# Sums of squares for eight unit norms: one plain f32 product, or two rounded passes

## The chip, the cores and the metric

The kernel runs on one core of one Trainium2 chip. The metric is the device time of one execution in microseconds, the median of several runs; lower is better. TensorE (PE) multiplies, VectorE (DVE), ScalarE (ACT) and GpSimd (POOL) do element work, SyncE (SP) issues most of the loads. Each engine takes its instructions strictly in the order in which the program lists them, and engines wait for each other by semaphores.

## The reference, cut to what matters

The model is a trunk of two layers over 512 tokens of width 1024. In each layer a combined projection feeds three token mixers, among them a gated delta rule (branch B) with four heads of 128. Its queries and keys go through a short convolution and SiLU, and then each head's vector of each token is scaled to unit length:

```
def l2_norm(x):
    return x * rsqrt(sum(x * x, axis=-1) + EPS)
...
qkv = causal_conv_silu(concatenate([b_q, b_k, b_v]), gdn_conv)
qb = l2_norm(qb.reshape(bsz, seq, B_HEADS, B_HEAD_DIM))
kb = l2_norm(kb.reshape(bsz, seq, B_HEADS, B_HEAD_DIM))
```

Four heads of keys and four of queries make eight unit norms per layer, 16 in all. After them come the delta rule, the other mixers' work, the merge and a squared-ReLU MLP.

## The kernel before, in words

Activations lie transposed: channels on the 128 partitions, the 512 tokens along the free dimension. A head of keys or queries is thus one 128x512 tile, `qkv[:, j, :]`, with j from 0 to 7, and the sum over its 128 channels is a sum over partitions. TensorE does it: a 128x128 matrix of ones times the 128x512 tile of squares gives the sum in every partition at once.

The large products are split in three rounded passes. A weight slab (128x1024) is loaded by SP into `raw`, rounded to `w_hi` (type fp32r) by POOL (lines 1182 and 1183), and VectorE takes the rest `w_lo = raw - w_hi` (line 1081, the step named `lo`); activations have `a_hi` and `a_lo` alike. A product is then hi\*hi + hi\*lo + lo\*hi in fp32r (lines 1216 to 1218), 24 matmuls a slab. The unit norms were not split in this way: line 1357 multiplies plain f32 operands.

The order of all instructions is written out by `schedule()`. The part around the change is its `prefix`, listed by hand. After the convolutions it runs, on each engine in this order (a step does nothing on an engine that has no part in it):

- `unit_sq 0`, `unit_sq 1`, `decays` (a table load on ScalarE, then four small activations and five small VectorE operations), `lo 15`, `rot 0`, `lo 16`, `va_turn`, `gcum`;
- four rounds. Round 0 is `rot 1`, `lo 17`, `unit 0`, `unit_sq 2`, `unit 1`, `unit_sq 3`, `turn 0`, `rows`; rounds 1 and 2 are the same with `rot 2` and `rot 3`, `lo 18` and `lo 19`, units 2, 3 and 4, 5, squares 4, 5 and 6, 7, `turn 1` and `turn 2`; round 3 has the slab `cv 0`, `lo 20`, units 6 and 7, `rot 4`, `turn 3`, and then the slab `cv 1` follows.

What the steps do. `rot r`: TensorE multiplies a slab into a PSUM bank, VectorE multiplies it by a cosine table (line 2159), and ScalarE copies it with its halves exchanged, in four pieces (line 1734), after VectorE's cosine of the same slab. `unit_sq j`: ScalarE squares tile j into `sqs[:, j % 2, :]` (line 1741). `unit j`: TensorE's product (line 1357, waits for the square), ScalarE's Ln and Exp (lines 1749 and 1751), VectorE's multiplication of the tile by the result (line 2174). `turn r`: VectorE multiplies the exchanged copy by a sine table and adds (lines 2168 and 2170). `lo n` makes the `w_lo` of slab n, two slabs ahead; TensorE waits for it before slab n. Slab 15 is that of `rot 1`, 16 that of `rot 2`, 17 that of `rot 3`, 18 and 19 those of `cv 0` and `cv 1`.

`sig(ins, name)` lets an instruction count up a semaphore, and `own(name)` makes an engine wait until its own last instruction of that name has finished.

Of the kernel before, what the change touches and what calls it, by code (L numbers as in the profile page):

```python
# [22 lines left out]
F32R = mybir.dt.float32r  # L23
ALU = mybir.AluOpType
ACT = mybir.ActivationFunctionType
AX = mybir.AxisListType

P = 128
D = 1024
S = 512  # L30
# [8 lines left out]
EPS = 1e-6  # L39
# [645 lines left out]
def build(nc, ws, wo, wd, par, post, tab, x_in, out, rows_d, mt_d, x_d, xt_d):  # L685
    with ExitStack() as ctx:
        def sb(name, shape, dt=F32, where=ctx):
            return where.enter_context(nc.sbuf_tensor(name, shape, dt))
# [9 lines left out]
        def sem(name):  # L698
            if name not in sems:
                sems[name] = ctx.enter_context(nc.semaphore(name))  # L700
            return sems[name]

        def inc(name, n=1, times=1):
            counted[name] += n * times
            return sem(name), n

        def on(name, v, of=None):


            return sem(name), v + (per_layer[name] * (layer if of is None else of) if name in per_layer else before[name])  # L710
# [16 lines left out]
        sqs = sb("sqs", [P, 2, S])  # L727
# [4 lines left out]
        with ExitStack() as mix:  # L732
            qkv = sb("qkv", [P, CONVS, S], where=mix)
            qa = sb("qa", [P, H, S], where=mix)
            ka = sb("ka", [P, S], where=mix)
            va = sb("va", [P, ST, P], where=mix)
            iq = sb("iq", [P, H, S], where=mix)
            ik = sb("ik", [P, S], where=mix)
            oc = sb("oc", [P, H, S], where=mix)
            bw = sb("bw", [P, 10, S], where=mix)  # L740
            tabs2 = sb("tabs2", [P, NTAB - basics], where=mix)
            with ExitStack() as u:
                cqk = sb("cqk", [P, 4, S], where=u)
                cv = sb("cv", [P, ST, S], where=u)
                rp = sb("rp", [P, 2, S], where=u)
            with ExitStack() as u:
                sc = sb("sc", [P, S], where=u)
                work = sb("work", [P, S], where=u)
                rl = sb("rl", [P, 2, S], where=u)
                negb = sb("negb", [P, S], where=u)  # L750
                pr = sb("pr", [P, H, S], where=u)
                pt = sb("pt", [P, 2, S], where=u)
            with ExitStack() as u:
                y_hi = sb("y_hi", [P, H, S], F32R, where=u)
                y_lo = sb("y_lo", [P, H, S], F32R, where=u)
                mt = sb("mt", [P, 3, S], where=u)
# [16 lines left out]
        def T(name, i=0, w=None):  # L773
            a, n = TAB[name]
            w = w or n
            if a < basics:
                return tabs[:, a + i * w:a + (i + 1) * w]
            return tabs2[:, a - basics + i * w:a - basics + (i + 1) * w]
# [82 lines left out]
        def signals(eng, who):  # L861
            seen = seen_by[who]

            def sig(ins, name):
                seen[name] = seen.get(name, 0) + 1
                ins.then_inc(*inc(name))

            def own(name):

                eng.wait_ge(sem(name), seen[name])  # L870

            sig.seen = seen
            return seen, sig, own


        MT, AT = [bw[:, n, :] for n in range(ST)], [bw[:, ST + n, :] for n in range(ST)]
# [113 lines left out]
        def level_count(n, l):  # L990

            return (LEVELS - FIRST) * (n // 2) + l - FIRST + 1

        def drained(name):

            k, a = name[0], name[1:]
            if k == "gcum":
                return [("gc", 1)]
            if k == "unit":
                return [("unit_ln", a[0] + 1)]  # L1000
            if k == "misc_turn":
                return [("misc_in", 3)]
            if k == "va_turn":
                return [("va_in", 1)]
            if k == "rs":
                return [("ret_p", RET[a] + 1)]
            if k == "ro":
                return [("oc", a[0] + 1)]
            if k == "rows":
                return [("rows_T", 1)]  # L1010
            if k == "kk":
                return [("MT", a[0] + 1)]
            if k == "kq":
                return [("AT", a[0] + 1)]
            if k == "kn":
                return [("K", a[0] + 1)]
            if k == "vn":
                return [("vb", a[0] + 1)]
            if k == "p1":
                return [(f"P1{a[0] % 2}", level_count(*a))]  # L1020
            if k == "xx":
                return [(f"X{a[0] % 2}", (LEVELS - 1 - FIRST) * (a[0] // 2) + a[1] - FIRST + 1)]
            if k == "xt":
                return [(f"XT{a[0] % 2}", level_count(*a))]
            if k == "wT":
                return [("wTn", a[0])]
            if k == "v2":
                return [("vnew", a[0] + 1)]
            if k == "oT":
                return [("ob", a[0] + 1)]  # L1030
            if k == "st":
                return [("St", a[0] + 1)]
            if k == "il":
                return [("relu", LOGITS[a[0]] + a[1] + 1)]
            if k == "as":
                return [("smax", H * TURN[a[0]] + a[1] + 1)]
            if k == "pt":
                return [("pt", SPREAD[a[0]] + a[1] + 1)]
            if k == "ao":
                return [("oa", TURN[a[0]] + 1)]  # L1040
            if k == "fin":
                return [("fin_ln", FIN[a])]
            raise ValueError(name)
# [52 lines left out]
        with nc.Block() as block:  # L1096
# [53 lines left out]
            for layer in range(DEPTH):  # L1150
# [63 lines left out]
                def _(pe):  # L1214
# [46 lines left out]
                    def small_bank(name):  # L1261
                        b, _, before = MID[name]
                        if before is not None:

                            for s, v in drained(before):
                                pe.wait_ge(*on(s, v))
                        return psM[b]

                    def small_done(ins):
                        ins.then_inc(*inc("small_done", 1))  # L1270
# [81 lines left out]
                    def unit(j):  # L1352
                        if j == 0:
                            pe.wait_ge(kept["tables_in"], 16 * (layer + 1))
                        pe.wait_ge(*on("unit_sq", j + 1))
                        ps = small_bank(("unit", j))
                        small_done(pe.matmul(ps[:, :], T("ones"), sqs[:, j % 2, :], start=True, stop=True))

                    def cv_tiles(i, ts):
                        u = DENSE["cv", 0]  # L1360
# [310 lines left out]
                def _(act):  # L1671
                    seen, sig, own = signals(act, "act")
# [64 lines left out]
                    def unit_sq(j):  # L1737
                        if j >= 2:
                            mid(act, ("unit", j - 2))
                        act.wait_ge(*on("silu", j + 1))  # L1740
                        sig(act.activation(sqs[:, j % 2, :], qkv[:, j, :], ACT.Square), "unit_sq")

                    def unit(j):
                        ps = mid(act, ("unit", j))
                        if j >= 2:
                            act.wait_ge(*on("unit_done", j - 1))
                        rt = gt[:, 2 + j % 2, :]

                        sig(act.activation(rt, ps[:, :], ACT.Ln, bias=4 * EPS), "unit_ln")
                        own("unit_ln")  # L1750
                        sig(act.activation(rt, rt, ACT.Exp, scale=-0.5,
                                           bias=0.0 if j < H else float(-0.5 * np.log(P))), "unit_r")

# [325 lines left out]
                def _(dve):  # L2079
                    seen, sig, own = signals(dve, "dve")  # L2080
                    total, rstd, diagonal, scaled = dve_norm(dve, sig, own)

                    def f32(ap):
                        return ap.bitcast(F32)
# [76 lines left out]
                    def turn(r):  # L2161
# [7 lines left out]
                        own("rot_sin")  # L2169
                        sig(dve.tensor_tensor(dst, dst, other, ALU.add), "rot_done")  # L2170

                    def unit(j):
                        dve.wait_ge(*on("unit_r", j + 1))
                        sig(dve.tensor_tensor(qkv[:, j, :], qkv[:, j, :], gt[:, 2 + j % 2, :], ALU.mult), "unit_done")

                    def rp_(h, m):
# [224 lines left out]
                    def merge(br, j):  # L2401
# [11 lines left out]
                        for i in range(2):  # L2413
# [2 lines left out]

                    steps = {"norm": norm, "conv": conv, "silu": silu, "misc_turn": misc_turn, "decays": decays, "gcum": gcum,
                             "rot": rot, "turn": turn,
                             "unit": unit, "rp": rp_, "lasts": lasts, "decay": decay, "vb": vb_, "MT": mt_, "AT": at_, "solve": solve,
                             "lev": lev, "Kp": kp_, "Kpp": kpp, "lvl": lvl, "X": x_, "XT": xt_, "Sd": sd, "St": st_,  # L2420
                             "lo": lambda n: lo_slab(dve, n), "index": index, "top": top, "smax": smax, "rinv": recip, "fin": fin,
                             "split": split_y,
# [266 lines left out]
```

## Time and profile before

| | |
|---|---|
| median of 3 runs | 1866.88 us (1866.54 to 1868.51) |
| the profiled execution's own time | 1864.98 us |
| its span, first to last instruction | 1862.8 us |
| busy: PE, DVE, ACT, POOL | 1836.6, 1249.1, 755.3, 265.4 us |
| granted TensorE clock, mean | 0.999 of full |

The profile comes from one execution. Times in it are microseconds from the first instruction. A row of a timeline gives the start, the length, the engine, line and operation, what it writes and reads, and how many instructions are merged in the row; brackets give the idle time of the engine ahead of it and what ended that. A matmul's length reaches into the next matmul, so the pace of matmuls is read from start to start. The same holds for short runs of ACT and DVE instructions that don't depend on each other.

### The profile page before, as it was taken

How to read it: one execution, taken by the hardware profiler on the slowest of the kernel's cores; microseconds unless marked ns; L12 is line 12 of the kernel's file. 1: busy time of each engine (PE TensorE's matmuls, PEld its weight loads, DVE VectorE, ACT ScalarE, POOL GpSimd, SP SyncE). 2: the span in 40 equal slices, each digit the busy share in tenths (PEclk: the TensorE clock that was granted, in tenths of full speed). 3: DMA queues.
4: the chain of work that ended last, by engine and by line, in shares of the span. 5: the costliest groups of instructions: out<-in, count | busy, mean ns of one | idle time of the engine just before them, and what ended most of it. 6: DMA issues, size and time to landing. Idle time of an engine off the chain costs nothing.

```text
span 1862.8 us, 23401 instructions
## 1 busy us (share of the span) xinstructions
PE 1836.6 (99%) x8622; PEld 1484.5 (80%) x8622; DVE 1249.1 (67%) x2064; ACT 755.3 (41%) x1261; POOL 265.4 (14%) x385
## 2 busy tenths in 40 slices
PE   8999999999999999999999999999999999999998
PEld 6877767888888888888778777678887888888886
DVE  6856789854475667575878658897534756575758
ACT  3163343421334636354531533524213346354454
POOL 2221111111120010000012211111112200100000
PEclk9999999999999999999999999999999999999999
DMA  6432213322341794766532322133224308857654
GB/s 247 139 125 85 69 57 99 82 84 68 132 162 46 208 256 133 206 177 174 161 108 91 128 70 79 58 99 86 68 80 176 140 24 239 235 141 198 186 142 102
DMA packets 87039, 240.32 MB, mean 129 GB/s; under 512 B 19920, under 2 KB 32400, under 8 KB 85904
## 3 DMA queue, kind: packets, MB, share of 16 engines
q1 hardware_dynamic: 46656, 171.89, 27.0%
q0 software_dynamic: 10368, 37.75, 10.9%
q10 hardware_dynamic: 29904, 29.19, 4.7%
q8 instruction: 70, 1.15, 0.2%
q14 instruction: 41, 0.34, 0.1%
HBM read 227.75 MB, written 11.06 MB: 128 GB/s over the span
## 4 chain that ended last, share of the span: by engine, by line
PE 90%; DVE 3%; ACT 3%; issue 1%; DMA 1%; ACTq 0%; POOL 0%; DVEq 0%; SPq 0%
PE psD L1216 23%; PE psD L1218 23%; PE psD L1217 23%; PE psM L1216 3%; PE psM L1217 3%; PE psM L1218 3%; PE psM L1275 2%; DMA d_raw<-in_wd 1%; PE psM L1289 1%; PE psM L1484 1%; PE psM L1282 1%; PE psM L1502 1%; PE psM L1381 1%; PE psM L1490 1%; PE psM L1373 1%
## 5 line engine op out<-in xcount | busy, mean ns | idle before, releaser
L1216 PE MATMUL psD<-a_hi,w_hi 128*128 128x512 f32 (+2 forms) x1488 | 594.0, 399 | 0.9 <-DVE w_lo L1081 0.6
L1218 PE MATMUL psD<-a_hi,w_lo 128*128 128x512 f32 (+2 forms) x1488 | 575.2, 387 | 0.0
L1217 PE MATMUL psD<-a_lo,w_hi 128*128 128x512 f32 (+2 forms) x1488 | 574.1, 386 | 0.0
L1081 DVE TENSOR_TENSOR w_lo<-raw,w_hi 128x1024 fp32r<-128x1024 f32 x216 | 264.4, 1225 | 141.3 <-POOL w_hi L1183 96.6
L1216 PEld LDWEIGHTS psD<-a_hi,w_hi 128*128 128x128 f32 (+1 forms) x1488 | 279.0, 188 | 77.8 <-issue 21.1
L1218 PEld LDWEIGHTS psD<-a_hi,w_lo 128*128 128x128 f32 (+1 forms) x1488 | 278.8, 187 | 58.0
L1217 PEld LDWEIGHTS psD<-a_lo,w_hi 128*128 128x128 f32 (+1 forms) x1488 | 279.3, 188 | 56.4 <-issue 4.3
L2496 DVE TENSOR_TENSOR d_lo<-d_raw,d_hi 128x1024 fp32r<-128x1024 f32 x102 | 124.1, 1222 | 69.6 <-ACT d_hi L2029 68.3
L1183 POOL TENSOR_SCALAR w_hi<-raw 128x1023 fp32r<-128x1023 f32 x150 | 166.4, 1109 | 0.0
L1182 POOL TENSOR_TENSOR w_hi<-raw,tabs 128x1 fp32r<-128x1 f32 x150 | 34.7, 231 | 902.6 <-PE psD L1218 871.6
L1190 POOL DMA_DIRECT2D d_raw<-in_wd x72 | 63.4, 956 | 642.7 <-DMA d_raw<-in_wd 435.8
L2029 ACT CAST d_hi<-d_raw 128x1024 fp32r<-128x1024 f32 x102 | 106.0, 1047 | 104.7 <-PE psM L1218 42.7
L2015 ACT CAST w_hi<-raw 128x1024 fp32r<-128x1024 f32 x62 | 65.1, 1050 | 84.1 <-PE psD L1218 83.5
L1216 PE MATMUL psM<-d_hi,f_hi 128*128 128x512 f32 x240 | 94.3, 393 | 0.1
L1218 PE MATMUL psM<-d_hi,f_lo 128*128 128x512 f32 x240 | 93.4, 389 | 0.0
L1217 PE MATMUL psM<-d_lo,f_hi 128*128 128x512 f32 x240 | 93.4, 389 | 0.0
L1931 ACT ACTIVATE gt<-psD 128x512 f32<-128x512 f32 x32 | 19.1, 597 | 159.6 <-PE psD L1218 147.8
L1734 ACT COPY wide<-psD 32x512 f32<-32x512 f32 (+1 forms) x84 | 48.6, 579 | 78.9 <-DVE iq L2159 34.5
L1216 PE MATMUL psD<-y_hi,w_hi 128*128 128x512 f32 x192 | 76.5, 399 | 0.0
L1218 PE MATMUL psD<-y_hi,w_lo 128*128 128x512 f32 x192 | 74.8, 389 | 0.0
L1217 PE MATMUL psD<-y_lo,w_hi 128*128 128x512 f32 x192 | 74.7, 389 | 0.0
L2023 ACT CAST f_hi<-gt 128x768 fp32r<-128x768 f32 x64 | 60.6, 947 | 29.1 <-DVE gt L2484 27.9
(297 smaller groups left out, 2875.7 us busy)
## 6 DMA issues: line engine op xcount, KB each, us to landing
raw<-in_ws SPq DMA_DIRECT2D x216, 512.0 KB, 3.4
d_raw<-in_wd SPq DMA_DIRECT2D x88, 512.0 KB, 5.7
d_raw<-in_wd POOLq DMA_DIRECT2D x72, 512.0 KB, 8.8
s_raw<-in_wo ACTq DMA_DIRECT2D x14, 512.0 KB, 11.5
tabs<-in_tab SPq DMA_DIRECT2D x2, 2944.0 KB, 12.1
x<-rows_d ACTq DMA_DIRECT2D x4, 1024.0 KB, 5.8
x<-out ACTq DMA_DIRECT2D x2, 2048.0 KB, 8.1
x<-in_x SPq DMA_DIRECT2D x4, 512.0 KB, 5.1
```

What stands on the lines that cost most here:

```text
L1081: dve.tensor_tensor(w_lo[:, s, :], raw[:, s, :], w_hi[:, s, :].bitcast(F32), ALU.subtract) \
L1183: pool.tensor_scalar(w_hi[:, s, 1:], raw[:, s, 1:], 1.0, 1.0, ALU.mult, ALU.mult) \
L1190: pool.dma_start(home(name), down_slab(c, b, j), accum_op=ALU.add).then_inc(*inc("sum_" + name[:None if name[0] == "C" else 1], 16))
L1216: pe.matmul(out, lhi, rhi, start=start, stop=False, skip_group_check=more)
L1217: pe.matmul(out, lhi, rlo, start=False, stop=False, skip_group_check=more)
L1218: return pe.matmul(out, llo, rhi, start=False, stop=stop, skip_group_check=more)
L1275: ins = pe.matmul(ps[:, cut(h)], lhs(h), rhs(h), start=True, stop=True)
L1734: sig(act.copy(wt[to:to + n, 6 + r % 2, :], src[at:at + n, :]), "rot_copy" if to + n == P else "rot_part")
L2015: act.copy(w_hi[:, s, :], raw[:, s, :]).then_inc(sem("w_hi"), 1)
L2023: sig(act.copy(f_hi[:, p, w, :], fr[:, w, :]), "f_hi" + part)
L2029: sig(act.copy(operand(c, st)[0], source(st)), "d_hi")
L2496: sig(dve.tensor_tensor(lo, source(st), f32(hi), ALU.subtract), "d_lo")
```

## The change

The squares are split like the other operands, and the sum is made in two passes with a rounded matrix of ones.

- ScalarE: behind each square, after waiting for it, a cast of the squares to `sq_hi` (fp32r). Both count on `unit_sq`.
- VectorE: a new step `unit_sq` in the place that the order already had for it: it waits for the cast and subtracts, `sq_lo = sqs - sq_hi`. Once per layer it also copies the ones to `ones_r`.
- TensorE: `unit j` waits for `sq_lo` of j, and then multiplies `ones_r` by `sq_hi` and by `sq_lo` into the same bank.
- The new tiles lie where `cv` and `rp` lie later. The Ln now counts on the same semaphore as the Exp (`unit_r`), and the waits' numbers follow.

```
+                sq_hi = sb("sq_hi", [P, 2, S], F32R, where=u)
+                sq_lo = sb("sq_lo", [P, 2, S], F32R, where=u)
+                ones_r = sb("ones_r", [P, P], F32R, where=u)
...
             if k == "unit":
-                return [("unit_ln", a[0] + 1)]
+                return [("unit_r", 2 * a[0] + 1)]
...
                     def unit(j):
-                        pe.wait_ge(*on("unit_sq", j + 1))
+                        pe.wait_ge(*on("unit_lo", j + 2))
                         ps = small_bank(("unit", j))
-                        small_done(pe.matmul(ps[:, :], T("ones"), sqs[:, j % 2, :], start=True, stop=True))
+                        pe.matmul(ps[:, :], ones_r[:], sq_hi[:, j % 2, :], start=True, stop=False)
+                        small_done(pe.matmul(ps[:, :], ones_r[:], sq_lo[:, j % 2, :], start=False, stop=True))
...
                         sig(act.activation(sqs[:, j % 2, :], qkv[:, j, :], ACT.Square), "unit_sq")
+                        own("unit_sq")
+                        sig(act.copy(sq_hi[:, j % 2, :], sqs[:, j % 2, :]), "unit_sq")
...
+                    def unit_sq(j):
+                        dve.wait_ge(*on("unit_sq", 2 * j + 2))
+                        if j == 0:
+                            sig(dve.tensor_copy(ones_r[:], T("ones")), "unit_lo")
+                        sig(dve.tensor_tensor(sq_lo[:, j % 2, :], sqs[:, j % 2, :], f32(sq_hi[:, j % 2, :]), ALU.subtract),
+                            "unit_lo")
+
                     def unit(j):
-                        dve.wait_ge(*on("unit_r", j + 1))
+                        dve.wait_ge(*on("unit_r", 2 * j + 2))
```

## Rows read from the trace of the kernel before

**Rows 1.** The page: busy time of each engine; engines on the last chain.
```profile
PE 1836.6 (99%) x8622; PEld 1484.5 (80%) x8622; DVE 1249.1 (67%) x2064; ACT 755.3 (41%) x1261; POOL 265.4 (14%) x385
...
PE 90%; DVE 3%; ACT 3%; issue 1%; DMA 1%; ACTq 0%; POOL 0%; DVEq 0%; SPq 0%
```

**Rows 2.** PE's waits, whole span: total us, times, longest us.
```profile
PE psM L1357 <- ACT sqs L1741: 1.1, 2, 0.5
...
PE psD L1216 <- DVE w_lo L1081: 0.6, 2, 0.3
```

**Rows 3.** Timeline of PE, layer 0, from rot 1 to units 6 and 7.
```profile
100.58 0.47 PE L1216 MATMUL psD<-a_hi,w_hi 128*128 128x512 f32 x1 [0.31 <-DVE w_lo L1081]
...
113.23 0.39 PE L1218 MATMUL psD<-a_hi,w_lo 128*128 128x512 f32 x1
113.46 1.88 PE L1357 MATMUL psM<-sqs,tabs 128*128 128x512 f32 x4
...
115.40 0.39 PE L1217 MATMUL psD<-a_lo,w_hi 128*128 128x512 f32 x1
...
129.76 1.13 PE L1357 MATMUL psM<-sqs,tabs 128*128 128x512 f32 x2 [0.54 <-ACT sqs L1741]
```

**Rows 4.** Timeline of ACT, layer 0: the first squares, then one round.
```profile
95.31 1.14 ACT L1741 ACTIVATE sqs<-qkv 128x512 f32<-128x512 f32 x2
96.47 1.28 ACT L1700 ACT_TABLE_LOAD   x1
...
107.06 2.39 ACT L1734 COPY wide<-psD 32x512 f32<-32x512 f32 x4 [2.99 <-DVE cqk L2159]
109.47 0.60 ACT L1749 ACTIVATE gt<-psM 128x512 f32<-128x512 f32 x1
110.10 0.63 ACT L1751 ACTIVATE gt<-gt 128x512 f32<-128x512 f32 x1
110.64 0.61 ACT L1741 ACTIVATE sqs<-qkv 128x512 f32<-128x512 f32 x1
111.16 0.58 ACT L1749 ACTIVATE gt<-psM 128x512 f32<-128x512 f32 x1
...
112.31 0.62 ACT L1741 ACTIVATE sqs<-qkv 128x512 f32<-128x512 f32 x1
...
115.09 2.38 ACT L1734 COPY wide<-psD 32x512 f32<-32x512 f32 x4 [2.03 <-DVE cqk L2159]
```

**Rows 5.** Timeline of DVE, layer 0: decays, lo 15, end of round 0, turn 1.
```profile
98.46 0.17 DVE L2136 SCALAR_TENSOR_TENSOR small<-small 128x16 f32<-128x16 f32 x1 [2.33 <-ACT small L1706]
...
99.21 1.22 DVE L1081 TENSOR_TENSOR w_lo<-raw,w_hi 128x1024 fp32r<-128x1024 f32 x1
...
112.43 0.69 DVE L2174 TENSOR_TENSOR qkv<-qkv,gt 128x512 f32<-128x512 f32 x1 [0.97 <-ACT gt L1751]
113.04 0.69 DVE L2168 TENSOR_TENSOR wide<-wide,tabs 128x512 f32<-128x512 f32 x1
...
114.37 0.68 DVE L2159 TENSOR_TENSOR cqk<-psD,tabs 128x512 f32<-128x512 f32 x1
...
121.80 1.42 DVE L2170 TENSOR_TENSOR cqk<-cqk,wide 128x512 f32<-128x512 f32 x1
```

**Rows 6.** Tile y_hi: a cast and a subtraction; ns min/median/max, first and last start.
```profile
L1897 ACT CAST y_hi<-oc x8: 613/616/619, 378.3 to 1304.9; 128x512 fp32r<-128x512 f32 x8
...
L2373 DVE TENSOR_TENSOR y_lo<-oc,y_hi x8: 684/686/694, 379.0 to 1305.9; 128x512 fp32r<-128x512 f32 x8
```

**Rows 7.** Timeline of POOL: rounding of slab 19.
```profile
121.17 1.51 POOL L1183 TENSOR_SCALAR w_hi<-raw 128x1023 fp32r<-128x1023 f32 x1
```

**Rows 8.** Timeline of PE: the kernel's first products; the same at layer 1's start.
```profile
7.78 2.08 PE L1072 MATMUL psM<-wide,x 128*128 128x128 f32 x8 [7.78 <-DVE wide L850]
...
938.02 1.16 PE L1072 MATMUL psM<-wide,x 128*128 128x128 f32 x8 [3.51 <-DVE wide L850]
```

**Rows 9.** Busy time by stretch: PE, PEld, DVE, ACT, POOL, granted clock, DMA, GB/s.
```profile
932.00:940.00 8.00, 4.26 (x35) 4.07 (x36) 6.53 (x21) 4.30 (x13) 0.00 (x0) 1.00 0.61 243
```

More of the change, by code:

```diff
@@ L746, in build @@
             with ExitStack() as u:
+                sb("cqk_place", [P, 4, S], where=u)
+                sq_hi = sb("sq_hi", [P, 2, S], F32R, where=u)
+                sq_lo = sb("sq_lo", [P, 2, S], F32R, where=u)
+                ones_r = sb("ones_r", [P, P], F32R, where=u)
+            with ExitStack() as u:
                 sc = sb("sc", [P, S], where=u)
@@ L1747, in unit @@
                         rt = gt[:, 2 + j % 2, :]
-                        sig(act.activation(rt, ps[:, :], ACT.Ln, bias=4 * EPS), "unit_ln")
-                        own("unit_ln")
+                        sig(act.activation(rt, ps[:, :], ACT.Ln, bias=4 * EPS), "unit_r")
+                        own("unit_r")
                         sig(act.activation(rt, rt, ACT.Exp, scale=-0.5,
@@ L2418, in _ @@
                              "rot": rot, "turn": turn,
-                             "unit": unit, "rp": rp_, "lasts": lasts, "decay": decay, "vb": vb_, "MT": mt_, "AT": at_, "solve": solve,
+                             "unit_sq": unit_sq, "unit": unit, "rp": rp_, "lasts": lasts, "decay": decay, "vb": vb_, "MT": mt_, "AT": at_, "solve": solve,
                              "lev": lev, "Kp": kp_, "Kpp": kpp, "lvl": lvl, "X": x_, "XT": xt_, "Sd": sd, "St": st_,
```

## The prediction, on record before the change was run

> **What bounds the kernel now.** I read the page first: TensorE is busy 1836.6 of 1862.8 us, and 90% of the last chain is on it [rows 1]. So a TensorE microsecond saved counts only where TensorE doesn't wait, and a wait added to TensorE costs its full length. Next the waits of TensorE: the unit product (line 1357) already waited for the square, 1.1 us in two places, at most 0.5 each, and the slab product for `w_lo`, 0.6 us in two [rows 2]. Two equal waits in a program of two layers: one in each. The timelines place them. Units 6 and 7: the square of unit 7 came 0.54 us late [rows 3]. The slab of rot 1 came 0.31 late, behind `lo 15` on VectorE [rows 3].
>
> That this stretch is no stretch of TensorE alone is seen from ACT. The four copies of rot 1 start at 107.06, those of rot 2 at 115.09 [rows 4]: a round takes 8.03. TensorE needs less: units 2 and 3 start at 113.46 and the second matmul of the next slab at 115.40, one pace of 113.46 - 113.23 = 0.23 behind the first [rows 3], so two units take 115.40 - 0.23 - 113.46 = 1.71, and a slab 24 x 0.23 = 5.5; together 7.2. So ACT and DVE turn in a closed loop that is longer than TensorE's round: copies, Ln, Exp, Square, Ln, Exp, Square on ACT [rows 4], then unit 1, turn 0 and the cosine on DVE (112.43 to 115.05 [rows 5]), which releases the next copies. TensorE had a small lead at first and had lost it by unit 7.
>
> **The change part by part.**
>
> *TensorE.* A unit in plain f32 costs 1.71 / 2 = 0.86; two fp32r passes at the slab's pace cost 0.46. That is 0.40 less, 6.4 over 16 units, if nothing waits. One fp32r pass at its length of 0.39 instead of its pace (nothing overlapped) would leave 0.08 of the 0.40; I take the pace, since the passes follow each other as in a slab.
>
> *ScalarE, before the table load.* The first two squares, the table load (96.47, no gap ahead of it) and the small activations stand in one row; DVE's decays wait for the last of them (98.46), `lo 15` follows at 99.21, and rot 1 starts when it is done [rows 3 to 5]. Each of two casts now goes in ahead of the load. The same form, 128x512 fp32r from f32, takes 0.616 [rows 6]; a dependent instruction starts 0.03 behind its forerunner's end (Ln 109.47 + 0.60, Exp 110.10 [rows 4]). So 0.64 each, 1.28 in all, and TensorE, which was already waiting there, idles 1.28 more. The two subtractions and the copy of the ones on DVE fall into the idle 2.33 ahead of 98.46 [rows 5], which the casts lengthen: nothing. Without that cover they would cost two times 0.69.
>
> *ScalarE, in the rounds.* Each cast again pushes what is behind it by 0.64, between 0.52 (the start-to-start time of Square and Ln that don't depend on each other, 110.64 to 111.16 [rows 4]) and 0.64; the wait of ACT for its own square makes it the latter.
>
> *VectorE, in the rounds.* `sq_lo` has the form of `y_lo`, 0.69 [rows 6], and its wait stands ahead of work: behind `sq_lo` of squares 3 are queued turn 0, the cosine of rot 2 and `lo 18`; the copies of rot 2 wait for the cosine. Before, turn 0 began 0.61 after unit 1, which began at the end of the second Exp (112.43, 113.04 [rows 5]). Now it begins 0.61 after `sq_lo`, and that one begins when the second cast ends: from the second Exp's start, 0.54 (110.10 to 110.64, Exp to Square), 0.64 and 0.62 instead of the Exp's own 0.63: +1.17. With the first cast's 0.64 the loop grows by 1.81 a round.
>
> *The walk through one layer.* The cosine of rot 2 comes 1.28 + 1.81 = 3.09 late. TensorE ends rot 2 at 113.46 + 1.28 - 0.80 (units 0 and 1, whose squares are ready) = 113.94, but `sq_lo` of square 3 ends at 112.31 + 0.62 + 1.28 + two casts 1.28 + 0.04 + 0.69 = 116.2, so TensorE stands for about 1.8 us between units 2 and 3. Round 1 adds 1.81: 4.90. In round 1 the add of turn 1 took 1.42 instead of 0.69, alongside POOL's rounding from 121.17 to 122.68, and ended 0.54 after that [rows 5, 7]. POOL follows TensorE's slabs and DVE now runs later against them, so this stretch goes: -0.73, and 4.17. But the end of rot 2 near 114.1 now puts POOL's next rounding (POOL start 0.2 behind a slab's end, 1.06 unstretched) on unit 1's product, 112.43 + 1.28 + 0.64 = 114.35: by the pattern of that row it ends at about 115.4 + 0.54 = 115.9 instead of 115.0, and `sq_lo` starts 0.35 later than 115.52. Then 4.52. Unit 7 in round 2 waits for two casts and one subtraction more than before: 0.64 + 0.64 + 0.73. It starts 6.53 later than 129.76, and saves its own 0.40: cv 1 starts 6.1 later. Of the 6.4 that the passes save, only these two last units' 0.8 is left; the rest is spent waiting. For both layers 12.3, bounds 2 x 5.8 (no stretch at all) and 2 x 6.9 (rot 2's and the old one).
>
> Here a rule bears on the added subtractions. The Trainium skill, "SBUF — State Buffer", section "SBUF: two separate sides", says that a VectorE operation with two SBUF inputs and a GpSimd operation that reads SBUF take a shared pair of ports by an exclusive lock, and whichever comes second is blocked for the other's whole instruction. The trace agrees: the add waited until POOL's 1.51 us were over [rows 5, 7]. By that rule the sum is 12.3; without it 11.6.
>
> *What is behind.* TensorE is nearly never idle after the stretch, so nothing takes the 12.3 back: the later stages start from the same order, all engines late by about the same.
>
> The sum: 1864.98 of the profiled execution + 12.3 = 1877.3. That execution lies 1.9 below the median of the runs, 1866.88; the forecast for the median is 1866.88 + 12.3 = 1879.2.
>
> **The rivals.**
>
> *The passes save what they promise (faster).* If `sq_lo` of squares 3, 5 and 7 were there when TensorE's slab ends, the kernel would gain 16 x 0.40 = 6.4: 1860.5. The point that decides is 113.94 for square 3, and the chain above gives 116.2; it would have to be 2.3 us shorter, more than both casts and the subtraction together can lose. For it speaks only TensorE's share of 99% [rows 1]. 5%.
>
> *The delay is regained (no change).* TensorE's wait for the square is 1.1 us in all [rows 2], and TensorE's idle time over the whole span is 26 us [rows 1]; what of it hangs on another engine could shrink. But 7.8 of it lies before the first product and 3.5 between the layers behind TensorE's own work [rows 8]. 1866.9; 4%.
>
> *Part of it.* The casts run closer (0.52), or rot 3 and cv 0 find ACT further ahead than I walk it: 4 us a layer, 1875 or somewhat below. 8%.
>
> *The clock.* TensorE stands twice in each of three rounds. Should the granted clock fall from 2.4 to 1.2 GHz, products take twice as long: the first eight of the kernel took 2.08, the same eight at layer 1's start 1.16 [rows 8], so 0.9 us are lost over eight such products; I take twice that, 1.8, for one fall. In the rounds the waits would cover this; behind unit 7 nothing does: +1.8 a layer, 1882.7. Against it: in the 8 us between the layers TensorE was busy 4.26 us, with a wait of 3.51, and the granted clock stayed 1.00 [rows 8, 9]. The Trainium skill, "TensorE: Matmul & The Clock Gate", part 1, says that idle time throttles TensorE back to half rate; these rows show none. 7%.
>
> **How the numbers follow.** My forecast has 76%, its own range 1875.5 to 1882. The range for 8 in 10 takes in most of the clock's case and the upper part of the third: 1874 to 1883.5. A measurement of this kernel tells 0.2%, 3.7 us, from no change; the forecast is 0.66% above. Slower: 76 + 7 + 8 = 91%; within: 4%; faster: 5%.
>
> **What would show it.** Right: the slab of rot 1 starts near 101.9 instead of 100.58 and waits for `w_lo` 1.6; TensorE waits for the new subtraction before units 3, 5 and 7 about 1.8 each, and somewhat less before 4 and 6; ACT's copies of rot 2 start near 118.5; cv 1's slab 6 us later; casts 0.62, subtractions 0.69, some up to 1.4 beside POOL; the pair of passes 0.46. Wrong: TensorE without waits in this stretch, or the same lateness at cv 1 but not at the end of the layer, or a granted clock below 1.00 in it.

## The result, and the profile after

The changed kernel takes 1885.62 us (median of 4 executions, 1884.31 to 1886.38), the kernel before took 1867.29 beside it (4 executions). The ratio is 1.0094, 95% interval 1.0081 to 1.0107. The change makes the kernel 18.3 us slower; forecast were 12.3, and the range ended at 1883.5. The profiled execution took 1885.68 (span 1883.8, mean granted clock 0.992 against 0.999), 20.7 above that of before.

The page, busy time of each engine, to be laid beside [rows 1]:

```profile
PE 1842.4 (98%) x8622; PEld 1492.3 (79%) x8622; DVE 1262.8 (67%) x2082; ACT 765.4 (41%) x1277; POOL 262.4 (14%) x385
```

Casts and subtractions appear as 10 us more on ACT and 14 on DVE. TensorE, which was to lose 6.4 us of work, shows 6 more: part of its work ran at half pace. Its waits, whole span (total, times, longest, in us), beside [rows 2]:

```profile
PE psM L1362 <- DVE sq_lo L2184: 12.4, 8, 1.9
PE psM L1077 <- DVE wide L855: 11.4, 2, 7.8
PE psD L1221 <- DVE w_lo L1086: 2.3, 2, 1.1
PE psM L1344 <- DVE small L2147: 2.1, 2, 1.1
```

The first, third and fourth add up to 16.8 us; the first and third were 1.7 in [rows 2]. They have places; the timeline of TensorE, layer 0 (start, length, and in brackets the wait ahead), beside [rows 3], the last row as in [rows 8]:

```profile
101.72 0.37 PE L1344 MATMUL psM<-small,tabs 128*128 128x16 f32 x2 [1.06 <-DVE small L2147]
...
103.22 0.47 PE L1221 MATMUL psD<-a_hi,w_hi 128*128 128x512 f32 x1 [1.14 <-DVE w_lo L1086]
103.99 0.40 PE L1221 MATMUL psD<-a_hi,w_hi 128*128 128x512 f32 x1
104.22 0.47 PE L1222 MATMUL psD<-a_lo,w_hi 128*128 128x512 f32 x1
104.49 0.63 PE L1223 MATMUL psD<-a_hi,w_lo 128*128 128x512 f32 x1
104.92 0.63 PE L1221 MATMUL psD<-a_hi,w_hi 128*128 128x512 f32 x1
...
110.41 0.39 PE L1362 MATMUL psM<-sq_hi,ones_r 128*128 128x512 f32 x1
110.63 0.39 PE L1363 MATMUL psM<-sq_lo,ones_r 128*128 128x512 f32 x1
110.86 0.39 PE L1362 MATMUL psM<-sq_hi,ones_r 128*128 128x512 f32 x1
...
127.61 0.50 PE L1362 MATMUL psM<-sq_hi,ones_r 128*128 128x512 f32 x1 [1.89 <-DVE sq_lo L2184]
...
129.40 0.80 PE L1362 MATMUL psM<-sq_hi,ones_r 128*128 128x512 f32 x1 [1.06 <-DVE sq_lo L2184]
...
140.16 0.50 PE L1362 MATMUL psM<-sq_hi,ones_r 128*128 128x512 f32 x1 [1.43 <-DVE sq_lo L2184]
...
948.11 2.07 PE L1077 MATMUL psM<-wide,x 128*128 128x128 f32 x8 [3.51 <-DVE wide L855]
```

The end of rot 1 in the kernel before, by its timeline of TensorE, is where unit 0 starts:

```profile
106.14 1.45 PE L1357 MATMUL psM<-sqs,tabs 128*128 128x512 f32 x3
```

Three things are to be seen. The pair of passes takes 110.86 - 110.41 = 0.45, as forecast. The slab of rot 1 begins at the full pace (104.22 - 103.99 = 0.23) and from its third product goes at 104.92 - 104.49 = 0.43: it takes until 110.41, 7.19 us, where the kernel before took 106.14 - 100.58 = 5.56. And the first products of layer 1 start 948.11 - 938.02 = 10.1 later than in [rows 8], behind the same wait of 3.51, but take 2.07 instead of 1.16. That this is the clock, the stretches say (PE, PEld, DVE, ACT, POOL busy, granted clock, DMA share, GB/s), beside [rows 9]:

```profile
94.00:104.00 10.00, 7.80 (x38) 6.29 (x37) 6.05 (x13) 5.62 (x12) 2.46 (x4) 1.00 0.16 53
104.00:108.00 4.00, 4.00 (x12) 3.15 (x11) 0.89 (x2) 2.61 (x5) 0.00 (x0) 0.57 0.79 250
...
128.00:134.50 6.50, 5.44 (x14) 4.05 (x13) 3.90 (x6) 3.68 (x7) 0.00 (x0) 0.52 0.84 325
...
944.00:952.00 8.00, 4.49 (x24) 4.30 (x23) 4.72 (x15) 3.16 (x9) 0.00 (x0) 0.72 0.45 180
```

0.52 to 0.57 of 2.4 GHz is, nearly, the level of 1.2 GHz. It fell after TensorE's waits of 1.06 and 1.14 with two small products between them, after waits of 1.89 and 1.06 at units 4 and 5, and at the border of the layers. Not every wait was followed by a fall: in layer 1 the same waits of 1.06 and 1.14 (at 1038.73 and 1040.24) were followed by a clock of 1.00 (1040 to 1048 us), and so was one of 1.84 at unit 3 of layer 0 (120 to 124 us).

ScalarE of after, beside [rows 4]: the first squares with their casts, then the first row of copies of rounds 0, 1 and 2.

```profile
95.83 0.62 ACT L1747 ACTIVATE sqs<-qkv 128x512 f32<-128x512 f32 x1
96.48 0.62 ACT L1749 CAST sq_hi<-sqs 128x512 fp32r<-128x512 f32 x1
...
98.31 1.28 ACT L1706 ACT_TABLE_LOAD   x1
...
111.33 2.39 ACT L1740 COPY wide<-psD 32x512 f32<-32x512 f32 x4 [4.63 <-DVE cqk L2167]
...
121.45 2.39 ACT L1740 COPY wide<-psD 32x512 f32<-32x512 f32 x4 [2.78 <-DVE cqk L2167]
...
131.31 2.38 ACT L1740 COPY wide<-psD 32x512 f32<-32x512 f32 x4 [2.69 <-DVE cqk L2167]
```

The third copies of the kernel before, by its timeline of ACT, so that both rounds can be compared:

```profile
123.85 1.18 ACT L1734 COPY wide<-psD 32x512 f32<-32x512 f32 x2 [2.90 <-DVE cqk L2159]
```

Round 0 grew from 8.03 to 121.45 - 111.33 = 10.12, round 1 from 123.85 - 115.09 = 8.76 to 9.86.

VectorE of after, beside [rows 5], with POOL's roundings behind it, beside [rows 7]:

```profile
100.60 0.97 DVE L2147 SCALAR_TENSOR_TENSOR small<-small 128x16 f32<-128x16 f32 x1
...
101.85 1.22 DVE L1086 TENSOR_TENSOR w_lo<-raw,w_hi 128x1024 fp32r<-128x1024 f32 x1
...
116.21 0.69 DVE L2184 TENSOR_TENSOR sq_lo<-sqs,sq_hi 128x512 fp32r<-128x512 f32 x1 [0.48 <-ACT sq_hi L1749]
117.37 1.51 DVE L2189 TENSOR_TENSOR qkv<-qkv,gt 128x512 f32<-128x512 f32 x1 [0.47 <-ACT gt L1759]
...
138.52 1.59 DVE L2184 TENSOR_TENSOR sq_lo<-sqs,sq_hi 128x512 fp32r<-128x512 f32 x1 [0.48 <-ACT sq_hi L1749]
```

```profile
100.50 1.05 POOL L1188 TENSOR_SCALAR w_hi<-raw 128x1023 fp32r<-128x1023 f32 x1
...
117.29 1.06 POOL L1188 TENSOR_SCALAR w_hi<-raw 128x1023 fp32r<-128x1023 f32 x1
...
138.51 1.06 POOL L1188 TENSOR_SCALAR w_hi<-raw 128x1023 fp32r<-128x1023 f32 x1
```

Three DVE operations in these rows overlap POOL's roundings and are long for it: a 128x16 operation of decays (0.97, where one of the same form takes 0.17 in [rows 5]), unit 1's multiplication (1.51), and `sq_lo` of square 7 (1.59). A fourth, `sq_lo` of square 4, took 1.23. This is the lock of the two engines' shared ports that the forecast took from the Trainium skill, "SBUF — State Buffer", section "SBUF: two separate sides"; the traces agree with it down to an operation of 16 columns. Over all 16 (min, median, max in ns):

```profile
L1749 ACT CAST sq_hi<-sqs x16: 617/620/625, 96.5 to 1073.2; 128x512 fp32r<-128x512 f32 x16
...
L2184 DVE TENSOR_TENSOR sq_lo<-sqs,sq_hi x16: 677/693/1591, 97.3 to 1073.9; 128x512 fp32r<-128x512 f32 x16
```

### The profile page after: what moved, and what is told of

It is laid out like the page before. It is cut to its first block, busy times and chain, and to the rows that moved or that the text cites. A ratio compares the mean times of both kernels' runs of the same rounds, so it can differ in the third digit from the quotient of the medians.

```text
span 1883.8 us, 23435 instructions
## 1 busy us (share of the span) xinstructions
PE 1842.4 (98%) x8622; PEld 1492.3 (79%) x8622; DVE 1262.8 (67%) x2082; ACT 765.4 (41%) x1277; POOL 262.4 (14%) x385
## 4 chain that ended last, share of the span: by engine, by line
PE 90%; DVE 4%; ACT 3%; issue 1%; DMA 1%; DVEq 0%; POOL 0%; ACTq 0%; SPq 0%; POOLq 0%
PE psD L1221 23%; PE psD L1223 23%; PE psD L1222 22%; PE psM L1221 3%; PE psM L1223 3%; PE psM L1222 3%; PE psM L1280 2%; PE psM L1294 1%; PE psM L1490 1%; PE psM L1287 1%; DMA d_raw<-in_wd 1%; PE psM L1508 1%; PE psM L1387 1%; PE psM L1496 1%; PE psM L1379 1%
## 6 DMA issues: line engine op xcount, KB each, us to landing
s_raw<-in_wo ACTq DMA_DIRECT2D x14, 512.0 KB, 11.4
```

## The experiments

The theory: the 12.3 forecast are the longer loop of ScalarE and VectorE (the *chain*), and the rest is the clock, which falls because TensorE now waits. The rivals: the passes themselves are dearer than they look; the loop is simply longer than walked and the clock only follows. *The stretch* of a layer reaches from ScalarE's first square to TensorE's first product behind the slabs that follow unit 7 (`rp` with `cv`); *late* compares TensorE's starts with the profiled execution of before. The edits are shortened; `...` and comments stand for the rest. Each job ran the kernel before beside its kernels (medians 1867.66 to 1868.35); the forecast's sums start from 1864.98, one execution of it.

**Two passes without the low part.** ScalarE writes the squares rounded at once; no cast, no subtraction. The second pass repeats the high part, with ones of 0.5, so the low part is left out.

```
-  pe.wait_ge(*on("unit_lo", j + 2))
+  pe.wait_ge(*on("unit_lo", 1)); pe.wait_ge(*on("unit_sq", j + 1))
...
-  sig(act.activation(sqs...), "unit_sq"); own("unit_sq"); sig(act.copy(sq_hi..., sqs...), "unit_sq")
+  sig(act.activation(sq_hi..., ACT.Square), "unit_sq")
```

> Two rounded passes on TensorE without the chain ahead of them: ScalarE's Square writes fp32r directly, no cast and no subtraction, and the second pass multiplies the same rounded squares (ones halved), so the low part of the squares is left out. Theory (the loop of ScalarE and VectorE is the bound of this stretch, 8.0 us a round against 7.2 of TensorE): the faster product mostly waits, only the last unit's 0.4 us of each layer is gained: 1866.5 us (1865 to 1867.5). Rival (TensorE's 0.40 us for each of 16 units is worth its sum): 1860.9. Rival (the two passes are themselves what made the change slow): above 1880.

Measured: 1867.46, ratio 0.9997 (0.9988 to 1.0006). The passes alone gain nothing, as the theory had it: the traced stretches are 0.4 us shorter (layer 0) and 0.2 longer (layer 1) than before, and TensorE waits ahead of the unit product (the trace puts it down to no releaser):

```profile
PE psM L1363 <- issue: 4.9, 6, 1.0
```

**The plain f32 product behind the new waits**, the opposite half.

```
-  pe.matmul(ps, ones_r, sq_hi..., stop=False); small_done(pe.matmul(ps, ones_r, sq_lo..., start=False))
+  small_done(pe.matmul(ps[:, :], T("ones"), sqs[:, j % 2, :], start=True, stop=True))
```

> The changed kernel with the plain f32 product of ones and squares back on TensorE; the casts, subtractions and all new waits stay (their results are not multiplied). Theory (TensorE waits in this stretch, so what a unit takes there counts only for the last unit of each layer): 2 x 0.4 more than the changed kernel, 1886.4 us (1884.5 to 1888). Rival (TensorE's saving of 0.40 us a unit is in the measured time and only hidden by a larger loss): 1885.6 + 6.4 = 1892. Rival (the passes are the loss): 1872 or less.

Measured: 1885.30, ratio 1.0092 (1.0077 to 1.0107), within 0.3 of the whole change. The f32 product costs 0.40 more for each of 16 units, and the time is the same: casts, subtractions and waits carry the loss, and the passes' 6.4 count for next to nothing behind them. The equality to 0.3 is not exact: in this trace the clock was 1.00 in layer 1's stretch, 0.94 in the changed kernel, so some of what the f32 product costs may come back there.

**The first squares behind `decays` and `rot 0`.**

```
-  ("unit_sq", 0), ("unit_sq", 1), ("decays",), ("rot", 0), ("va_turn",),
+  ("decays",), ("rot", 0), ("unit_sq", 0), ("unit_sq", 1), ("va_turn",),
```

> The changed kernel with the first two squares, casts and subtractions moved from ahead of the decays to behind rot 0, so that ScalarE's table load and VectorE's w_lo for rot 1 come as early as before. Theory (each added instruction costs where it stands ahead of what TensorE waits for; 2.1 us a layer at rot 1 by the trace, and the fall of the clock in layer 0's rot 1 of 1.6 us that follows the wait): 1885.6 - 2 x 2.1 - 1.6 + some 0.5 for later squares of unit 1 = 1880.3. Rival (only the rounds count and take the time back): 1885. Rival (the clock alone is the cost, and falls wherever TensorE first waits): 1882 to 1885.

Measured: 1877.81, ratio 1.0053 (1.0038 to 1.0068), 7.8 below the change and 2.5 below what was expected. Layer 0 ends the stretch 5.1 late instead of 10.1. `decays` now runs before POOL's rounding, and its operation is short again (timeline of DVE):

```profile
97.98 0.18 DVE L2147 SCALAR_TENSOR_TENSOR small<-small 128x16 f32<-128x16 f32 x1
```

Taking the casts from the front of the prefix thus gives back their own 1.28, the collision's 0.8, and the clock's fall of 1.6 in rot 1 (1.00 from 100 to 108 us there). That is 3.7 of the 5.0; most of the rest is `sq_lo` of square 7, which took 0.68 there and not 1.59.

**Products that nobody reads, in TensorE's waits.** No step is moved and work is added, so a gain points to the clock.

```
+  fill(4)   # ahead of gcum, and ahead of the slab of rot 1
+  fill({3: 7, 4: 7, 5: 4, 7: 5}.get(j, 0))   # ahead of unit j; 128x512 products into a free bank
```

> The filled kernel again without the products between the layers, which stood behind the wait there, not in it, and took 6 us: only the fills ahead of gcum, rot 1 and units 3, 4, 5, 7. Theory (in the stretch the clock's falls cost what the traces of the changed and the filled kernel differ by: 3.0 us in layer 0, 0.4 in layer 1): clock 1.00 through both stretches, 1885.6 - 3.4 = 1882.2 (1880 to 1884). Rival (the falls are covered by waits): 1885 to 1886. Rival (keeping TensorE busy there lets the clock stay up at the layers' border too): 1879.

Measured: median 1884.77, ratio 1.0085 (1.0067 to 1.0103): a miss against what was expected, and undecided. Its four executions are 1878.77 (mean granted clock 0.999), 1883.92 (0.997), 1885.62 (0.995) and 1886.51 (0.996). The first is the profiled one; layer 0 leaves the stretch 6.9 late, layer 1 another 6.9, with a clock of 1.00 in both stretches and at the border. Why the others fell is not in a trace; the border's wait and units 2 and 6 were not filled.

**The same with the border filled too, in a wrong place**: 52 products stood behind the border's long wait, not in it.

```
+  if layer and t == ST - 1:   # fill as above, and 52 products 128x128 here
```

> The changed kernel, with TensorE's waits filled by products that nobody reads: 4 ahead of gcum, 4 ahead of rot 1, 7, 7, 4 and 5 ahead of units 3, 4, 5 and 7 (128x512 fp32r, 0.23 us each, each group shorter than the wait it stands in), and 52 of 128x128 in the wait between the layers. No step is moved. Theory (on top of the longer chain, the granted clock falls behind these waits: 1.6 us in layer 0's rot 1, 2.7 at the layers' border, and cv 0 at half pace in both layers, which puts POOL's next rounding onto a subtraction, 0.9 each): clock 1.00 in the stretch and 1885.6 - 1.6 - 2.7 - 1.8 = 1879.5. Rival (the clock's falls are covered by the waits, the chain alone is the cost): 1885 to 1886. Rival (the fill delays TensorE): above 1887.

Measured: 1893.47, ratio 1.0128 (1.0106 to 1.015): a miss. The added products cost their full length on TensorE in the traced execution:

```profile
947.14 6.00 PE L1094 MATMUL psD<-a_hi 128*128 128x128 f32 x52
```

The stretches of that trace still tell something: the clock was 1.00 in them, and each was 7.1 longer than before. But that execution took 1885.80; the other three took 1892.53 to 1895.05 at mean clocks of 0.993 to 0.996, so the clock fell in them somewhere for all the filling, and no trace shows where.

**The border alone**: 26 products ahead of its wait, nothing in the rounds.

```
+  if layer and t == 2:   # 26 products 128x128, into a bank that is written again behind them
```

> The changed kernel with 26 products of 128x128 that nobody reads (0.115 us each by the filled kernel's trace, 3.0 in all) ahead of the wait of 3.5 us between the layers; nothing in the rounds is touched. Theory (the granted clock falls at the border in this kernel, 3.0 us between layer 1's first and last transposition): 1885.6 - 2.9 = 1882.7 (1881 to 1884). Rival (the fall is covered there or follows from the stretch with the norms): 1885 to 1886.5.

Measured: 1886.96, ratio 1.01 (1.0087 to 1.0114): 1.3 above the change, where 2.9 below were expected. The border's fall is gone (timeline of TensorE, then layer 1's stretch in the columns of the stretches above):

```profile
944.52 3.10 PE L1094 MATMUL psD<-a_hi 128*128 128x128 f32 x26
...
948.28 1.16 PE L1077 MATMUL psM<-wide,x 128*128 128x128 f32 x8 [0.66 <-DVE wide L855]
```

```profile
1030.00:1090.00 60.00, 52.20 (x208) 41.02 (x207) 36.75 (x56) 36.24 (x68) 10.73 (x15) 0.91 0.31 104
```

The same products take 1.16 again. But layer 1's stretch was 8.9 longer than before in this trace, against 7.8 in the changed kernel's, at a clock of 0.91 (0.94 there). So the border alone gains nothing; the falls lay elsewhere in this trace, and their prices can't be added up singly. Whether filling the border moved them, or executions simply differ, one trace of each doesn't tell.

**Rounds and border both filled**, with units 2 and 6 as well.

```
+  fill({2: 1, 3: 7, 4: 7, 5: 4, 6: 7, 7: 5}.get(j, 0))   # and fill(4) twice, and the 26 at the border
```

> The changed kernel with the fills of the rounds, and besides 1 product ahead of unit 2, 7 ahead of unit 6 and the 26 at the layers' border, so that no wait of TensorE over 1 us is left from the first slab of layer 0 on. Theory (the chain of ScalarE and VectorE alone costs 14.1 us, which the filled kernel's one execution at clock 0.999 showed; what the other executions had above that are falls of the clock behind the waits that were left): all executions at a mean clock of 0.998 or 0.999, and 1864.98 + 14.1 = 1879 us (1877.5 to 1881). Rival (the falls are not tied to TensorE's waits): some executions again at 0.995 to 0.997 and 1884 to 1887. Rival (the fills themselves cost in the other executions): 1884 or more at a clock of 0.999.

Measured: 1880.81, as expected (5 executions, 1880.09 to 1881.72; clock 0.998 or 0.999 in each), ratio 1.0076 (1.0062 to 1.009). That is 4.8 below the change by the medians (3.4 by the ratios, whose intervals overlap at their ends; the executions' ranges don't overlap). TensorE's wait for `sq_lo`, and both stretches:

```profile
PE psM L1373 <- DVE sq_lo L2195: 1.7, 6, 0.3
```

```profile
94.00:150.00 56.00, 54.76 (x238) 42.84 (x237) 35.91 (x55) 36.21 (x67) 9.04 (x16) 1.00 0.30 104
...
1030.00:1090.00 60.00, 58.81 (x267) 46.56 (x266) 38.72 (x56) 36.06 (x68) 10.08 (x16) 1.00 0.31 106
```

How long a stretch is at that clock, the first square and the first product behind it show, in each layer; before (layer 0's first square is in [rows 4]):

```profile
170.28 1.02 PE L1381 MATMUL psM<-rp,cv 128*128 128x512 f32 x2
...
1020.18 1.14 ACT L1741 ACTIVATE sqs<-qkv 128x512 f32<-128x512 f32 x2
...
1095.14 1.02 PE L1381 MATMUL psM<-rp,cv 128*128 128x512 f32 x2
```

and with rounds and border filled:

```profile
95.97 0.62 ACT L1758 ACTIVATE sqs<-qkv 128x512 f32<-128x512 f32 x1
...
177.99 1.02 PE L1398 MATMUL psM<-rp,cv 128*128 128x512 f32 x2
...
1027.80 0.62 ACT L1758 ACTIVATE sqs<-qkv 128x512 f32<-128x512 f32 x1
...
1109.82 1.02 PE L1398 MATMUL psM<-rp,cv 128*128 128x512 f32 x2
```

That is 74.97 and 74.96 before, and 82.02 in both layers here. The traces of the two kernels above with filled rounds, with the clock at 1.00 as well, have 82.00 to 82.04 in all four of their stretches. So with the clock up the chain is worth 7.05 a layer, 14.1 in all. The changed kernel's stretches are 84.5 and 82.8, and the clock's falls make the difference. This tells the theory from the rival that the loop is merely longer and the clock's falls are covered by waits.

**`turn` ahead of the units of its round**, so that the next cosine and copies don't stand behind `sq_lo`.

```
+  prefix.append(("turn", r))
   for j in (2 * r, 2 * r + 1):
...
-  prefix.append(("turn", r))
```

> The changed kernel with one step of VectorE moved: turn r (two operations, 1.33 us to the next start) ahead of units 2r and 2r+1, where it runs beside ScalarE's copies, and no longer between unit 2r+1 and the next cosine. Casts, subtractions and passes as they are. Theory (the closed loop of ScalarE and VectorE sets the pace; it shrinks by 1.33 a round in rounds 0 and 1, ahead of unit 7's wait): 1885.6 - 2 x 2 x 1.33 = 1880.3 (1877.5 to 1882). Rival (TensorE's own work or the clock sets the pace): 1884.5 to 1887.

Measured: 1879.93, ratio 1.0064 (1.0049 to 1.0079), 5.7 below the change, as expected. Not all of it is the change's loss: the same move gives 2.9 in the kernel before (the next run), so about half of the 5.7 is left for what `sq_lo` ahead of `turn` on VectorE adds. The waits for `w_lo` (2.3) and for `decays` (2.1) are as long as in the change.

**The same order in the kernel before**, the only edit to it.

```
+  prefix.append(("turn", r))   # ahead of the round's units, not behind them
```

> The kernel before with only turn r moved ahead of the units, plain f32 product and nothing of the change. Theory (the move shortens a loop that had just overtaken TensorE's round; 8.0 - 1.3 = 6.7 a round is below TensorE's 7.2, so only the wait of 0.54 at unit 7 of each layer can go): about 1.1 below the kernel before, 1867 us (1866 to 1868). Rival (the move is itself worth the 5 to 6 us that it gave in the other two kernels): 1862.

Measured: 1865.47, ratio 0.9984 (0.9975 to 0.9993): 2.9 better, half a microsecond more than the range expected; its traced layer 0 is 1.1 earlier. This execution had a granted clock of 0.997, and its border (as [rows 8, 9]) reads

```profile
937.16 2.08 PE L1072 MATMUL psM<-wide,x 128*128 128x128 f32 x8 [3.50 <-DVE wide L850]
```

```profile
932.00:940.00 8.00, 4.50 (x28) 4.31 (x28) 5.68 (x19) 3.60 (x11) 0.00 (x0) 0.76 0.57 229
```

The clock falls here without any of the change. In [rows 8] the same wait of 3.51 was followed by 1.16; that execution was one in which it held. Of the twelve traces in which nothing fills this wait, nine show a fall behind it (the eight products or the 16 behind them take longer), and three show none: that of before and those of the two kernels with filled rounds whose border is not filled ahead of the wait.

**Squares, casts and subtractions early, in the convolutions**, where ScalarE and VectorE have room, in 16 tiles of their own.

```
+  if 2 <= j < 2 * H + 2: prefix.append(("unit_sq", j - 2))
+  if 3 <= j < 2 * H + 3: prefix.append(("unit_lo", j - 3))
...
-  if j + 2 < 2 * H: prefix.append(("unit_sq", j + 2))
```

> All of the change's instructions, but in another place: the squares, casts and subtractions of all eight heads go into the convolutions' stretch, one head behind each SiLU, into sixteen tiles that are free there (those of bw, oc and qa); the rounds keep only the product, Ln, Exp and the multiplication. Theory (the added work costs only because it stands in the closed loop of ScalarE and VectorE): TensorE waits for no square any more, its passes' 6.4 us come back in part, until VectorE's later steps (w_lo of the fourth cv slab) hold it: 1863 us (1860 to 1866). Rival (the added instructions or the two passes cost by themselves): 1880 to 1886. Rival (the convolutions' stretch has no room on VectorE, which is busy four fifths of it): 1870 to 1880.

Measured: 1864.40, ratio 0.998 (0.997 to 0.999). TensorE still waited for ScalarE (3.5 in all) and `w_lo` (2.2).

**Early, and `turn` first**: both edits.

```
+  prefix.append(("turn", r))   # ahead of the units, with the early steps above
```

> The kernel with early squares, casts and subtractions, with turn r moved ahead of the units as well. In the trace of the early kernel TensorE still waited 1.77 us at cv 0 for ScalarE's copies and 1.08 at the fourth cv slab for w_lo, in each layer. Theory (both hang on the same loop, now 6.2 us a round against TensorE's 6.4): both waits go, 1864.4 - 2 x 2.85 = 1858.7 (1857 to 1861), which would be the two passes' 6.4 us in full and some more. Rival (the next thing on VectorE takes their place): 1862 to 1864.5.

Measured: 1857.95, ratio 0.9947 (0.993 to 0.9964). TensorE has no wait left in the stretch:

```profile
94.00:150.00 56.00, 56.00 (x264) 46.70 (x263) 35.61 (x58) 31.09 (x58) 11.18 (x18) 1.00 0.39 137
```

**The same order with the plain f32 product**: early squares, no casts, no subtractions.

```
-  pe.matmul(ps, ones_r, hi8[j], stop=False); small_done(pe.matmul(ps, ones_r, lo8[j], start=False))
+  small_done(pe.matmul(ps, T("ones"), <square of j>, start=True, stop=True))
```

> The fastest kernel so far (early squares, turn first) with the plain f32 product on squares that are kept in f32, so without casts, subtractions and the second pass. Theory (where TensorE waits for no square, its 0.40 us a unit are worth their sum): 1857.95 + 6.4 = 1864.3 us (1863 to 1866). Rival (the gain came from the moved steps and the passes are worth nothing): 1857 to 1860.

Measured: 1864.01, ratio 0.9977 (0.9968 to 0.9986). The passes are worth 6.1 between these two kernels, near the 6.4 of the forecast's first term: they pay as soon as the squares are there.

**Early, `turn` first, two passes, and the border filled.**

```
+  if layer and t == 2:   # the 26 products of above
```

> Early squares, turn first, and the 26 products at the border. Theory (the same fall of the clock at the border is in this kernel's executions, whose mean clock is 0.997; its trace shows 1.6 us more there than the kernel before): 1857.95 - 1.6 = 1856.3 (1855 to 1857.5). Rival (the clock is not the border's): 1857.5 to 1859.

Measured: 1856.95 (1855.58 to 1858.09), ratio 0.994 (0.9928 to 0.9953), the fastest of all, 11.4 below the kernel before; the last 1.0 of it is not told from nothing.

## Why the prediction failed

**What held.** The direction, and the longer chain as its main cause. The pair of passes takes 0.45 (forecast 0.46), the casts 0.62, the subtractions 0.69. The loop of ScalarE and VectorE grew as walked: round 0 by 2.09 (forecast 1.81 + 0.35 for POOL's rounding on unit 1), round 1 by 1.10 (1.81 - 0.73). The predicted collision on unit 1 is there, with 1.51. TensorE's saving is spent waiting, as the f32 product behind the same waits shows. What is lost in layer 0 is carried to its end unchanged, 10.1 at the first products of layer 1.

**Where the 10.1 of layer 0 differ from the 6.1.** At the copies of rot 3 the walk has 4.52; measured are 131.31 - 123.85 = 7.46. Of the difference 0.5 lies ahead of the stretch (squares at 95.83 instead of 95.31; the same program up to there gave -0.2 to 1.5 between traces). 0.8 is the collision of `decays`: the casts' 1.28 pushed it onto POOL's rounding of 100.50, 0.97 instead of 0.17, and `lo 15` and rot 1 behind it. The walk moved `decays` by 1.28 and didn't look what POOL does then. 1.6 is rot 1 at half pace (7.19 instead of 5.56). The last 0.9 comes behind these copies: `sq_lo` of square 7, 1.59 instead of 0.69, beside POOL's rounding, which follows a slab that ran at half pace. Where that slab ran at full pace (rounds and border filled), the same rounding fell on `sq_lo` of square 6, 1.28, and `sq_lo` of square 7 took 0.69.

**The step that failed: the clock's rival.** The sum had the clock's falls at nothing, and they cost 5.9 in the profiled execution; as a rival they had 7% and 1.8 a layer, since "in the rounds the waits would cover this" and "these rows show none". Both were wrong, and a granted clock below 1.00 in the stretch, which the forecast had named as a sign of being wrong, is what came. Rot 1's slab is ahead of the copies and hence in the loop: a slower slab shifts all that follows. And [rows 8, 9] show one execution in which the clock held behind a wait of 3.51; in the trace of the kernel before with only `turn` moved, the same wait is followed by a clock of 0.76, it falls there in nine of twelve traces, and nine executions of before in the job of the last filling have mean clocks of 0.996 to 0.999, the two lowest times (1864.01, 1864.68) at 0.999. "These rows show none" was a sample of one. The Trainium skill, "TensorE: Matmul & The Clock Gate", part 1, which the forecast named and set aside, was right that idle time brings TensorE back to half rate: these traces agree, though not behind every wait. A second, smaller step of the sum was short: it moved `decays` without looking at POOL, 0.8 a layer.

**The sum by the runs.** In the profiled executions, 20.7: the chain 14.1 (two stretches of 7.05, measured with the clock at 1.00), falls of the clock 2.5 in layer 0 (1.6 + 0.9), 2.6 at the border (3.0, of which 0.4 is regained before the next stretch) and 0.8 in layer 1 (82.77 - 82.01; there `sq_lo` of square 7, at 1073.87, took 1.53 beside POOL's rounding, behind a slab that ran at 0.50 from 1064 to 1068 us), and 0.7 at start and end. The chain was forecast with 12.3; 1.6 of the missing 1.8 is the collision of `decays` in both layers. By the medians, the filled kernel puts the clock at 3.4 to 4.8 of the 18.3. The medians differ by less than the traces, probably because most executions of before lose something at the border too: their mean clocks are mostly below the 0.999 of the traced one, but no trace of before shows a fall.

**What stays open.** Why the clock falls in one execution, or one layer, and holds in another behind the same wait; why it fell more in layer 1 in the trace with the border filled; and where it fell in the executions of the two partly filled kernels that were not traced.

## What to carry to other kernels

Before work is put ahead of a table load or a rounding, look at what the *third* engine does at the moment into which the old work is pushed; a small operation under POOL's lock took over five times its length here (0.97 instead of 0.17), on the path. A wait added to TensorE is priced with what the clock does behind it: look at more than one execution, or fill every wait with products nobody reads and see whether the time falls (filling only some of them gave no clear gain here). And split work that feeds TensorE is best made long before it is needed: the change cost 18 us where TensorE waits for its casts and subtractions; made early, with `turn` moved ahead, the kernel is 10 us faster than before (1868.16 to 1857.95), of which moving `turn` alone gives 2.9.

## What had not been expected of the hardware

Two waits of 1.06 and 1.14 us with small products between were followed by a granted clock of 0.57 for 4 us in layer 0, and by 1.00 in layer 1 of the same execution. A single wait of 3.51 at the border was followed in some traces by eight products in 1.16, with the full pace behind them, and in others by the same eight in 1.24 to 2.08. With one place filled, the falls were found in another. An fp32r product of 128x128 took 6.00 / 52 = 0.115 us, half of the 0.23 of 128x512.
